# Gated delta core: the turn of a batch one round later, the diagonals of U by ScalarE, the first decays beside the last value groups, half tiles handed out anew

## What is computed

```
g = cumsum(g);  decay = exp(g_i - g_j) for i >= j
a = strict_lower((k*beta) k^T * decay)
t_inv = (I + a)^-1
u = t_inv v_beta;  w = t_inv (k_beta * exp(g))
qk = lower(q k^T * decay)
per chunk: v_new = u - w S;  o = (q*exp(g)) S + qk v_new
           S = S * exp(g_last) + k_tail^T v_new
o = o * rsqrt(mean(o^2)) * norm_w * silu(z);  result = o @ w_out
```

## Time and profile before

| | us |
|---|---|
| median of 3 runs (lowest, highest) | 1759.9 (1758.12, 1761.21) |
| the profiled execution's own time | 1759.94 |
| its span | 1758.2 |
| PE busy | 1665.4 (95% of the span) |
| DVE, ACT, POOL busy | 1013.6, 882.1, 179.2 |
| mean granted clock of PE | 0.968 |

### The profile page before, as it was taken

The page is one execution under the profiler, slowest core; times in us unless marked ns, Lnnn a source line. Parts: engine busy times, 40 slices in busy tenths (PEclk is TensorE's granted clock), DMA queues, the critical chain, the costliest instruction groups (busy, mean ns, idle before and its releaser), DMA issues.

```text
span 1758.2 us, 25819 instructions
## 1 busy us (share of the span) xinstructions
PE 1665.4 (95%) x10243; PEld 1370.6 (78%) x10243; DVE 1013.6 (58%) x1557; ACT 882.1 (50%) x1372; POOL 179.2 (10%) x184
## 2 busy tenths in 40 slices
PE   6999999999999999997988899999999799799998
PEld 5888888888888888775777788888877587678887
DVE  4555576655475555776444466555655545656663
ACT  5544455644364445664333355444667332356662
POOL 1000001000000001021232110000210200201220
PEclk9999999999999999998988899999989799899999
DMA  7555565655565555442211158555522122255542
GB/s 233 182 189 183 166 220 174 198 186 182 177 210 185 189 188 164 145 144 73 73 38 36 63 159 237 188 183 185 164 82 77 48 74 74 97 158 178 184 176 95
DMA packets 208634, 261.78 MB, mean 149 GB/s; under 512 B 21707, under 2 KB 145026, under 8 KB 208514
## 3 DMA queue, kind: packets, MB, share of 16 engines
q1 hardware_dynamic: 208514, 260.12, 46.3%
HBM read 259.01 MB, written 1.05 MB: 148 GB/s over the span
## 4 chain that ended last, share of the span: by engine, by line
PE 84%; DVE 9%; ACT 2%; POOL 2%; issue 2%; ACTq 0%; DVEq 0%; POOLq 0%
PE acc L452 23%; PE acc L454 23%; PE acc L453 23%; DVE low L427 3%; DVE gdn_cv L1317 2%; PE aux L2523 1%; ACT high L417 1%; PE tr L698 1%; PE aux L985 1%; DVE mix_S L2663 1%; PE tr L526 1%; PE tr L3276 1%; PE tr L1692 1%; PE aux L1000 0%; PE acc L2871 0%
## 5 line engine op out<-in xcount | busy, mean ns | idle before, releaser
L427 DVE TENSOR_TENSOR low<-raw,high 128x1024 fp32r<-128x1024 f32 (+1 forms) x487 | 591.4, 1232 | 437.9 <-ACT high L417 437.1
L417 ACT ACTIVATE high<-raw 128x1024 fp32r<-128x1024 f32 (+1 forms) x487 | 502.4, 1047 | 358.5 <-PE acc L454 343.8
L452 PE MATMUL acc<-high,xh 128*128 128x512 f32 (+1 forms) x1360 | 548.8, 404 | 7.1 <-DVE low L427 6.2
L454 PE MATMUL acc<-high,xl 128*128 128x512 f32 (+1 forms) x1360 | 531.3, 391 | 0.0
L453 PE MATMUL acc<-low,xh 128*128 128x512 f32 (+1 forms) x1360 | 530.7, 390 | 0.0
L452 PEld LDWEIGHTS acc<-high,xh 128*128 128x128 f32 x1360 | 259.9, 191 | 63.4 <-DVE low L427 7.3
L454 PEld LDWEIGHTS acc<-high,xl 128*128 128x128 f32 x1360 | 259.4, 191 | 53.9
L453 PEld LDWEIGHTS acc<-low,xh 128*128 128x128 f32 x1360 | 260.3, 191 | 48.3 <-issue 0.7
L452 PE MATMUL acc<-high,hh 128*128 128x512 f32 x472 | 185.9, 394 | 0.0
L454 PE MATMUL acc<-high,hl 128*128 128x512 f32 x472 | 184.1, 390 | 0.0
L453 PE MATMUL acc<-low,hh 128*128 128x512 f32 x472 | 183.9, 390 | 0.0
(11 more groups left out here) (448 smaller groups left out, 1748.1 us busy)
## 6 DMA issues: line engine op xcount, KB each, us to landing
raw<-in_ffn_w_gate_up SPq DMA_DIRECT2D x352, 256.0 KB, 3.1
raw<-in_ffn_w_down SPq DMA_DIRECT2D x176, 256.0 KB, 3.0
raw<-in_gdn_w_in SPq DMA_DIRECT2D x96, 256.0 KB, 2.9
raw<-in_ffn_up SPq DMA_DIRECT2D x88, 256.0 KB, 3.0
raw<-in_w_in SPq DMA_DIRECT2D x72, 256.0 KB, 2.9
raw<-in_sc_w_in SPq DMA_DIRECT2D x48, 256.0 KB, 3.1
raw<-in_ffn_down SPq DMA_DIRECT2D x44, 256.0 KB, 2.8
raw<-in_gdn_w_out SPq DMA_DIRECT2D x32, 256.0 KB, 2.9
```

The lines of the kernel that those rows point to most:

```text
L417: nc.scalar.activation(high[t % HIGHS][:, 0:n], raw[t % RAWS][:, 0:n], ACT.Copy).then_inc(high_ready, 1)
L427: nc.vector.tensor_tensor(low[t % RAWS][:, 0:n], raw[t % RAWS][:, 0:n], high[t % HIGHS][:, 0:n].bitcast(F32), ALU.subtract).then_inc(low_r ...
L452: nc.tensor.matmul(o, a, wh, start=(k0 + kk == 0), stop=False)
L454: mm = nc.tensor.matmul(o, b, wh, start=False, stop=(k0 + kk == k - 1))
```

## The change

It has five parts.
1. The turn of batch B is in round B+2 at positions 6 and 7 (before: round B+1, positions 9 and 10), ahead of decay, decay_turned and grams, which move to positions 8, 9 and 10. In round 0 they are at 4, 5 and 6 (before 0, 1 and 2). The turn of batch 2 is in LAST. The normed values stand one position behind the mean and ahead of grams_dve; scores_dve stands two positions behind grams_dve.
2. The diagonals of U are two ACT activations at position 11 (last_diag_act) in place of two GpSimd products.
3. The decay and decay_turned of batch 0 are four steps (first_decay_pe, first_decay_act), each half the size of a decay, in aux[1] in place of tr. They stand behind the pairs 10, 11, 12 and 13. GpSimd's spread for them is in the loop at g = 5.
4. FILL and LAST are new. Half tiles ahead of round 0: 1, 2 and 1 at the pairs and 2 behind the grams (before 1, 2, 2, then 1 and 1); in the rounds 8, 9, 9 and 8 (before 7, 6, 6 and 6); in LAST 8 (before 16).
5. place alternates from one group to the next by what the last one had, not by the number of the group. The product with w_out has banks 0, 1 and 2, 3, as before.

Waits go with the moves: values0_pe and state_pe wait for grams_dve and scores_dve of the next batch, turn_pe for the last output. The diff, with the edits for ACT and DVE that say the same as PE's left out in places:

```diff
@@ -346,8 +346,12 @@
     place.append([0, 1])
+elif g[0] == "gdn_out":
+    place.append([2 * (gi - first["gdn_out"]) + t for t in range(TB)])
 else:
-    place.append([2 * (gi % 2) + t for t in range(TB)])
+    low_pair = gi == 0 or 2 in place[-1] or 3 in place[-1]
+    place.append([0, 1] if low_pair else [2, 3])
@@ -1052,8 +1056,9 @@
-FILL = ((0, 0, 0, 1, 1, 1, 1, 1, 1, 1, 0, 0, 0),) + 3 * ((1, 1, 1, 1, 0, 0, 1, 1, 0, 0, 0, 0, 0),)
-LAST = (2, 2, 2, 2, 0, 2, 2, 2, 2)
+FILL = ((1, 1, 1, 1, 1, 1, 1, 0, 0, 0, 0, 1, 0),) + 2 * ((1, 1, 1, 1, 0, 1, 1, 1, 0, 0, 1, 1, 0),) + (
+    (1, 1, 1, 1, 0, 0, 0, 0, 1, 1, 1, 1, 0),)
+LAST = (1, 1, 1, 1, 1, 1, 1, 1, 0)
 def __init__(self):
@@ -1360,19 +1366,20 @@
         self.pairs_pe(pe, 2 * g - 2)
+        if g >= 6:
+            self.first_decay_pe(pe, 2 * (g - 6))
...
         self.pairs_pe(pe, 2 * g - 1)
+        if g >= 6:
+            self.first_decay_pe(pe, 2 * (g - 6) + 1)
     fill = self.fill_pe(pe)
-    for s, n in ((14, 1), (15, 2), (16, 2)):
+    for s, n in ((14, 1), (15, 2), (16, 1)):
...
         self.pairs_pe(pe, s)
-    self.decay_pe(pe, 0)
-    self.some(fill, 1)
-    self.decay_turned_pe(pe, 0)
     self.grams_pe(pe, 0)
-    self.some(fill, 1)
+    self.some(fill, 2)
@@ -1474,8 +1481,9 @@
             self.pairs_pool(pool, 2 * g - 1)
-    self.spread_pool(pool, 0)
-    self.inv.pool(pool, 0)
+        if g == 5:
+            self.spread_pool(pool, 0)
+            self.inv.pool(pool, 0)
@@ -1490,8 +1498,6 @@
             self.gate_pool(pool, R - 1)
-        if R < self.NB:
-            self.last_pool(pool, R)
@@ -1513,9 +1519,10 @@
                 yield
-    pe.wait_ge(self.g_U_corner, 2 * self.NB)
...
     for t in body[:8]:
+        if t == body[4]:
+            pe.wait_ge(self.g_U_corner, 2 * self.NB)
@@ -1570,6 +1577,7 @@
         self.last_act(act, B)
+        self.last_diag_act(act, B)
 def inverse_dve(self, dve, B, i):
@@ -1596,6 +1604,13 @@
         yield
+    else:
+        for _ in range(2):
+            yield
+    for h in range(2):
+        if R >= 2:
+            self.turn_pe(pe, R - 2, h)
+        yield
@@ -1605,10 +1620,6 @@
     yield
-    if 0 < R < self.NB:
-        for h in range(2):
-            self.turn_pe(pe, R - 1, h)
-            yield
 def other_act(self, act, R):
@@ -1623,19 +1634,22 @@
         yield
+    else:
+        for _ in range(2):
+            yield
+    for h in range(2):
+        if R >= 2:
+            self.turn_act(act, R - 2, h)
+        if R and h == 0:
+            self.square_act(act, R - 1)
+        yield
...
         self.decay_act(act, R + 1)
-    if R:
-        self.square_act(act, R - 1)
...
     yield
-    if 0 < R < self.NB:
-        for h in range(2):
-            self.turn_act(act, R - 1, h)
-            yield
 def other_dve(self, dve, R):
@@ -1650,21 +1664,54 @@
         yield
-    yield
+    else:
+        for _ in range(2):
+            yield
+    for h in range(2):
+        if R >= 2:
+            self.turn_dve(dve, R - 2, h)
+        if R and h:
+            self.mean_dve(dve, R - 1)
+        yield
     if R:
-        self.mean_dve(dve, R - 1)
+        self.normed_dve(dve, R - 1)
+    yield
...
         self.grams_dve(dve, R + 1)
-    if R:
-        self.normed_dve(dve, R - 1)
+    yield
+    yield
...
     yield
-    if 0 < R < self.NB:
-        for h in range(2):
-            self.turn_dve(dve, R - 1, h)
-            yield
+def first_decay_pe(self, pe, i):
+    a = i % 2
+    pe.wait_ge(self.g_gm_ready, 8)
+    if i == 0:
+        pe.wait_ge(self.g_t3out, 8)
+    elif i == 1:
+        pe.wait_ge(self.g_D_ready, 1)
+    else:
+        pe.wait_ge(self.g_D_ready, 2)
+        pe.wait_ge(self.g_DT_ready, a)
+    if i < 2:
+        mm = nc.tensor.matmul(aux[1][:, :], upto[:, :], self.gm[:, 4 * a:4 * a + 4, :].rearrange("p j s -> p (j s)"), start=True, stop=True)
+    else:
+        for j in range(4):
+            mm = nc.tensor.matmul(aux[1][:, j * P:(j + 1) * P], self.gm[:, 4 * a + j, :], upto[:, :], start=True, stop=True)
+    mm.then_inc(self.g_D_psum if i % 2 else self.g_D_half, 1)
+def first_decay_act(self, act, i):
+    a = i % 2
+    if a:
+        act.wait_ge(self.g_D_psum, i // 2 + 1)
+    else:
+        act.wait_ge(self.g_D_half, i // 2 + 1)
+    dst = (self.A if i < 2 else self.qk)[0][:, 4 * a:4 * a + 4, :].rearrange("p j s -> p (j s)")
+    nc.scalar.activation(dst, aux[1][:, :], ACT.Exp).then_inc(self.g_D_ready if i < 2 else self.g_DT_ready, 1)
@@ -1680,14 +1727,14 @@
 def decay_pe(self, pe, B):
     pe.wait_ge(self.g_gm_ready, 8 * B + 8)
-    if B == 0:
-        for u in (self.unit + 14, self.unit + 15):
-            pe.wait_ge(tr_free[u % 2], u // 2 + 1)
-    elif B == 1:
+    if B == 1:
...
         pe.wait_ge(self.g_o_ready, B - 1)
+    if B >= 3:
+        for u in (self.zunit + 2 * B - 6, self.zunit + 2 * B - 5):
+            pe.wait_ge(tr_free[u % 2], u // 2 + 1)
@@ -1783,13 +1832,13 @@
-def last_pool(self, pool, B):
+def last_diag_act(self, act, B):
     if B:
-        pool.wait_ge(self.g_v1_psum, B)
-    pool.wait_ge(self.inv.u_ready, self.inv.all_done(B))
+        act.wait_ge(self.g_v1_psum, B)
+    act.wait_ge(self.inv.u_ready, self.inv.all_done(B))
     for f in range(2):
-        nc.gpsimd.tensor_scalar(self.U[:, :, 64 * f:64 * f + 64], self.Uc[B % 2][:, :, :], lohi[:, f:f + 1], None,
-                                ALU.mult).then_inc(self.g_U_diag, 1)
+        nc.scalar.activation(self.U[:, :, 64 * f:64 * f + 64], self.Uc[B % 2][:, :, :], ACT.Copy,
+                             scale=lohi[:, f:f + 1]).then_inc(self.g_U_diag, 1)
@@ -1797,12 +1846,13 @@
 def values0_pe(self, pe, B):
...
     pe.wait_ge(self.g_U_corner, 2 * B + 2)
-    if B:
-        for u in (self.zunit + 2 * B - 2, self.zunit + 2 * B - 1):
+    if B + 1 < self.NB:
+        pe.wait_ge(self.g_A_ready, 8 * B + 16)
+    else:
+        for u in (self.zunit + 2 * B - 4, self.zunit + 2 * B - 3):
             pe.wait_ge(tr_free[u % 2], u // 2 + 1)
-    else:
-        pe.wait_ge(self.g_A_ready, 16)
-        pe.wait_ge(self.g_qk_ready, 2)
+        pe.wait_ge(self.g_o_ready, B)
@@ -1824,6 +1874,7 @@
 def state_pe(self, pe, B):
     pe.wait_ge(self.g_vt_ready, 4 * B + 4)
+    pe.wait_ge(self.g_qk_ready, min(B + 2, self.NB))
@@ -1924,9 +1975,7 @@
 def turn_pe(self, pe, B, h):
     pe.wait_ge(self.g_o_gated, 2 * B + 2)
-    if B + 2 < self.NB:
-        pe.wait_ge(self.g_A_ready, 8 * (B + 3))
-        pe.wait_ge(self.g_qk_ready, B + 3)
+    pe.wait_ge(self.g_o_ready, min(B + 2, self.NB))
```

More of the change, by code:

```diff
@@ L1152, in __init__ @@
                 self.g_D_psum = sem("gdn_D_psum")
+                self.g_D_half = sem("gdn_D_half")
                 self.g_D_ready = sem("gdn_D_ready")
@@ L1398, in act @@
                         self.pairs_act(act, 2 * g - 2)
+                    if g >= 6:
+                        self.first_decay_act(act, 2 * (g - 6))
                     stream_act(act, gi)
@@ L1405, in act @@
                         self.pairs_act(act, 2 * g - 1)
+                    if g >= 6:
+                        self.first_decay_act(act, 2 * (g - 6) + 1)
                 fill = self.fill_act(act)
-                for s, n in ((14, 1), (15, 2), (16, 2)):
+                for s, n in ((14, 1), (15, 2), (16, 1)):
                     self.some(fill, n)
                     self.pairs_act(act, s)
-                self.decay_act(act, 0)
-                self.some(fill, 1)
-                self.decay_turned_act(act, 0)
-                self.some(fill, 1)
+                self.some(fill, 2)
                 for B in range(self.NB):
@@ L1652, in other_dve @@
                     yield
+                else:
[7 more added lines that the diff above has]
+                    yield
+                if R:
+                    self.normed_dve(dve, R - 1)
                 yield
-                if R:
-                    self.mean_dve(dve, R - 1)
                 yield
@@ L1722, in grams_pe @@
                     pe.wait_ge(self.g_t3out, 8)
+                    for u in (self.unit + 14, self.unit + 15):
+                        pe.wait_ge(tr_free[u % 2], u // 2 + 1)
                 for a in range(2):
```

## The result

The changed kernel took 1749.6 us (median of 6 runs, 1747.2 to 1754.4), the kernel before 1761.0 on the same chip; the ratio is 0.9942, with a 95% interval of 0.9932 to 0.9952. It is faster, as forecast, by 11 us and not by 21. The profiled execution took 1748.78 us (span 1747.1), 11.2 less than the profiled one of before.

What follows compares the result with a forecast made beforehand. TensorE's waits and the low clock behind them were taken as the bound: 52.4 us. The new order would lose 31.2, so 21.2 gained from 1759.94 us gives 1738.7, stated as 1739; range 1730 to 1752.

Steps and rivals of the forecast that it cites:

- The turn: Batch B's turn, moved to round B+2: all 13.3 us of waits go, and the three low clocks behind them.
- The last turn: Batch 3's turn behind the last output: PE waits 4.0 us, then runs at the low clock, costing 2.3 us.
- First decays: Pairs ahead of round 0: Exp and table switches cost 5.9 us, low clock 2.3; the stretch loses 13.7 us.
- Round 0: Four uncovered steps at 0.62 us each, plus 0.9 for VectorE's queue: 3.4 us lost.
- rival C: The low clock stays on through round 3 and LAST, giving 1769 us; chance 0.07.
- Rounds 1 to 3: PE's waits, mostly on VectorE and ScalarE, lose 0.9, 1.5 and 4.2 us; values of batch 3 add 0.9 and 0.3.
- The matmuls themselves are the same: Whole core: 48 half tiles and the same batches, decays and turns, so new time is old minus 52.4 plus new losses.
- Diagonals: ScalarE's two copies at position 11 lie beside a half tile: 0 us; without the half tile 0.8 a round.
- banks: The new handing of banks to groups saves no wait: 0 us, bounds 0.6 either way.
- Rival A: In-order queues leave 0.25 us at each of 39 steps in rounds 1 to 3, 10 us: 1749 us; chance 0.20.

Runs made afterwards that it cites:

- e5_turnboth: Changed kernel with both halves of the last batch's turn at step 11 of the last products, not one each at 10 and 11; 1744.5 us, ratio 0.9910.
- e3_copy0: Changed kernel with the four first decays' exponentials replaced by copies with scale zero, so ScalarE loads no tables there; 1746.7 us, ratio 0.9925.
- e4_nofirst: Changed kernel with batch 0's decays behind the pairs again, two more half tiles there and one less in round 0; 1746.8 us, ratio 0.9925.
- e1_fill0: Changed kernel with round 0's seven half tiles redistributed: none at positions 4 to 6, three more at 7 to 9; 1746.4 us, ratio 0.9925.
- e2_dummy: Changed kernel with four small unread matmuls added at each of positions 7 to 10 of round 0; 1744.0 us, ratio 0.9909.
- e6_normed: Changed kernel with VectorE's normed scaling issued one position later in rounds 1 to 3, behind the copy of X; 1746.0 us, ratio 0.9920.
- e9_bdummy: Kernel before the change, with fourteen small matmuls put ahead of each of the turn's three mid-round waits for GpSimd; 1763.4 us, ratio 1.0013.
- e7_diagpool: Changed kernel with the diagonals of U written by GpSimd again at the end of its round, not by ScalarE; 1751.1 us, ratio 0.9951.
- e8_three: Changed kernel with the edits of e1_fill0, e5_turnboth and e6_normed together; 1734.9 us, ratio 0.9852.
- e10: Changed kernel with the old rule that gives groups their banks by the parity of the group; 1750.1 us, ratio 0.9941.
- e12: Like e11, with one half tile moved from behind the last pair back to position 11 of round 0; 1734.6 us, ratio 0.9851.
- e11: e8_three and e4_nofirst together, with no half tile at position 11 of round 0; 1733.7 us, ratio 0.9849.

## Why the prediction was partly right

The mechanism was right and the size was half: 11.2 us between the profiled executions for 21.2. The difference of 10.1 us is 8.1 more loss in the core (39.3 for 31.2), 3.4 more of busy time reckoned at the full clock (before 261.8 − 52.4 = 209.4, after 252.1 − 39.3 = 212.8), and 1.4 gained outside of the core that I did not forecast.

The 8.1 are nearly all low clock. The sum held 26.6 us of idle time, and 27.4 were measured. It held 4.6 us of low clock, 2.3 ahead of round 0 and 2.3 behind the last turn, and 11.9 were measured. So the waits were priced well, and the term that was mis-sized is the low clock of the new order, put at nothing in all four rounds (the range held 5 us for one in round 3).

- **The turn.** Right: no wait of the turn in rounds 2 and 3, and none of the low clocks behind them. The last turn waited 3.63 us (4.0 forecast), and 3.0 of low clock followed (2.3). e5_turnboth takes away 2.8 of the wait for nothing.
- **First decays.** Right in its terms: eight loads, the last Silu within 1.5 us, loss 14.4 for 13.7, low clock 2.8 for 2.3. (The terms that it names add up to 828.1 for round 0, not 827.8.) e3_copy0 gives 4.8 us for the loads, where my step had 4.9 of its 5.9 for them. e4_nofirst has the part itself cost 1 to 3 us.
- **Round 0, the step that failed most.** "Round 0: four steps have neither a half tile nor a part of another batch, 4 × 0.62 [...] 0.9 more: 3.4." The idle time is 3.35. But I put no low clock behind it, and it cost 3.9. The evidence that I used against rival C, 5.3 us of waits at 813 to 829 with the clock at 1.00, was of another arrangement. Here gaps of 1.36 and 0.61 us, with only small matmuls between and behind them, were followed by the fall, and two more gaps of 0.6 came at the low clock. e1_fill0 and e2_dummy show it from both sides. So rival C's mechanism exists, in one place and for some 10 us; that the clock would stay down through round 3 and behind did not happen.
- **Rounds 1 to 3.** Idle 0.7, 2.6 and 5.3 for 0.9, 1.5 and 5.4 (with the values of batch 3). Round 3 had the pieces differently spread: one wait of 2.42 for VectorE's X, where I had 1.3 and 1.6 in two places; with 1.45 of low clock it was 1.4 over. e6_normed shows that the queue order was the cause of the wait; the low clock is missing in e1_fill0 with the same wait. Round 2 was 1.1 over.
- **"The matmuls themselves are the same": the other step that failed.** They are, but their price isn't. First, the low clock of before was overpriced: e9_bdummy gives 4.5 for the formula's 5.3, since small matmuls don't take twice as long at half the clock. For the 9.3 us of low clock that went (21.2 to 11.9 by the same formula) that is some 1.4 us, if the share of this stretch, 0.15, holds for all. Second, a half tile costs more between small matmuls than among its own kind. Round 2 at the full clock has 38.51 us of busy time with nine half tiles in the changed kernel, and in e9_bdummy, with six, 30.39 and 3.43 behind its turn's start, 33.8: that is 1.56 for each and not 1.36. The rounds have 34 half tiles for 25, so 1.8 us. Together 3.2 of the 3.4. Both are worked out and not tested: the second compares two kernels with different orders, and the ends of matmuls are modelled in a profile. The 1.4 us outside stay open; the stages behind the core alone read 716.6 to 721.2 us in the profiles of kernels that don't change them.
- **Diagonals and banks at 0.** The banks: shown. The diagonals: the time could not tell, but the profile of e7_diagpool has 2.2 us more of waits for GpSimd's copies (3.4 and 0.9 for 2.1), because they come behind the gate. In the kernel before PE itself waited for that gate product at the turn; that this hid the copies is argued, not tested. So ScalarE's copies may be a small gain that I had at 0.
- **Rival A**, 10 us of queueing spread over 39 steps, gives the right time by the wrong road. It would have some 10 us more idle time in rounds 1 to 3, and there are 8.6 for the 7.8 forecast. Of the 8.1 us too much loss 3.9 stand in one place, and three local edits took 13.4 us from the core.

## What to carry to other kernels

Price the low clock for each stretch of waits in the new order, not only for the long waits that go: two gaps of 1.36 and 0.61 us, with only small matmuls between, were enough here, and three half tiles moved by three positions took it away. When an engine with an ordered queue serves the critical one, look first at what stands ahead of the awaited instruction: one position for `normed_dve` and one step for the turn took 2.4 and 2.8 us of waiting away for nothing, and lowered the time by 3.9 and 5.6 us by the ratios. And a gain read as idle time plus low clock is an upper bound: round trips that the slow clock had covered open again. Before crediting a stretch of a single profile to an edit, look at the same stretch in profiles of kernels that don't touch it.

## What the runs showed of the hardware

- What the half clock costs in small matmuls: four 128x128 transposes go from 0.66 to 1.11 us (1.7 times), and a stretch of 6.98 us of such work from the full clock takes 11.50 at a mean of 0.54 (1.65 times, where the clock alone would make it 1.85).
- Filling a wait with useless matmuls pays only where they are short against the gaps. In e2_dummy 3.2 us of them gave a shorter round. In e9_bdummy those ahead of the first two turns (5.7 and 4.8 us) came too late in the wait and ran beyond it, and those ahead of the third (3.4 us) ran inside the wait and only put the low clock off by 4.8 us.
- The same instructions have their low clock in different places from one execution to the next. The pairs' stretch, unchanged in the kernels e1, e5 and e8, took 50.7, 50.7 and 53.4 us in their profiles (clocks 0.90, 0.90 and 0.84), 51.9 in the changed kernel. Round 3 with the values of batch 3 took 52.1 us in e1 (1.00) and 56.4 in e10 (0.91) with the same waits; the stages behind the core took 716.6 (e12) to 721.2 (e11). The runs of the changed kernel lie 7.2 us apart, those of e8_three 1.6.
